# RWKV mixer: whole-bank transposes of k, b and the output rows, and a reordered tail

## What is computed

```
def step(state, inp):                     # one token t of each of 16 heads of width 64
    r_t, w_t, k_t, v_t, a_t, b_t = inp
    sa = einsum('bhvk,bhk->bhv', state, a_t)
    state = state * w_t + sa[..., None] * b_t + v_t[..., None] * k_t
    y_t = einsum('bhvk,bhk->bhv', state, r_t)
...
y = group_norm(y) * ln_w + ln_b + bonus   # per head
return (y * g) @ w_o                      # g = sigmoid(xg @ g1) @ g2
```

## Time and profile before

| | us |
|---|---|
| runs of the kernel before | 1758.68, 1757.01, 1758.20 |
| their median | 1758.20 |
| the profiled execution | 1757.71 |
| its span in the trace | 1755.1 |
| the RWKV stage from x to the last group of w_o in that span | 1437.7 to 1561.7 |

### The profile page before, as it was taken

The page is one execution under the profiler, slowest core; times in us unless marked ns, Lnnn a source line. Parts: engine busy times, 40 slices in busy tenths (PEclk is TensorE's granted clock), DMA queues, the critical chain, the costliest instruction groups (busy, mean ns, idle before and its releaser), DMA issues.

```text
span 1755.1 us, 33424 instructions
## 1 busy us (share of the span) xinstructions
PE 1728.4 (98%) x12454; PEld 1523.5 (87%) x12454; DVE 1003.2 (57%) x1927; ACT 945.6 (54%) x1414; POOL 1133.0 (65%) x506
## 2 busy tenths in 40 slices
PE   8999999999999999999999999999999999999998
PEld 6888899999999999888888887988888989978887
DVE  5224333992478888544444446465555985665555
ACT  5468454446544444455444456666657762346565
POOL 6966776887888888655555556755566463555553
PEclk9999999999999999999999999999999999999999
DMA  8543443665544444566667763455544521245552
GB/s 303 195 157 130 159 173 141 184 184 181 175 148 141 140 143 143 168 192 192 192 207 253 242 191 108 169 216 192 191 150 138 178 63 52 66 156 194 190 190 83
DMA packets 68094, 292.57 MB, mean 167 GB/s; under 512 B 13184, under 2 KB 13712, under 8 KB 50464
## 3 DMA queue, kind: packets, MB, share of 16 engines
q1 hardware_dynamic: 67808, 291.12, 50.8%
q0 software_dynamic: 48, 0.08, 0.0%
q10 hardware_dynamic: 144, 0.07, 0.0%
HBM read 289.14 MB, written 1.05 MB: 165 GB/s over the span
## 4 chain that ended last, share of the span: by engine, by line
PE 80%; POOL 9%; issue 5%; ACT 2%; DVE 2%; DMA 1%; POOLq 0%; DVEq 0%; SPq 0%; ACTq 0%
PE bank L1060 8%; POOL rows_lo L2983 7%; PE bank L876 7%; PE bank L1081 6%; PE bank L938 6%; PE bank L941 6%; PE bank L935 6%; PE bank L1196 4%; PE bank L1064 4%; PE bank L882 4%; PE bank L618 4%; PE bank L624 4%; PE bank L619 4%; PE bank L908 3%; PE bank L647 1%
## 5 line engine op out<-in xcount | busy, mean ns | idle before, releaser
L2968 POOL TENSOR_TENSOR unit_lo<-unit_raw,unit_hi 128x2048 fp32r<-128x2048 f32 (+1 forms) x86 | 332.9, 3886 | 132.4 <-ACT unit_hi L1649 119.6
L2983 POOL TENSOR_TENSOR rows_lo<-rows_raw,rows_hi 128x1024 fp32r<-128x1024 f32 x128 | 309.6, 2420 | 84.8 <-ACT rows_hi L1769 46.0
L3010 POOL TENSOR_TENSOR a_lo<-table,a_hi 128x256 fp32r<-128x256 f32 x128 | 178.7, 1396 | 159.7 <-ACT a_hi L1848 159.6
L2567 DVE TENSOR_TENSOR rows_lo<-rows_raw,rows_hi 128x1024 fp32r<-128x1024 f32 x128 | 161.8, 1264 | 185.5 <-ACT rows_hi L1844 185.5
L1844 ACT ACTIVATE rows_hi<-rows_raw 128x1024 fp32r<-128x1024 f32 x128 | 135.6, 1060 | 168.4 <-PE bank L941 168.4
L3040 POOL TENSOR_TENSOR up_lo<-up_raw,up_hi 128x2048 fp32r<-128x2048 f32 x22 | 111.2, 5054 | 156.5 <-ACT up_hi L1920 126.9
L1649 ACT ACTIVATE unit_hi<-unit_raw 128x2048 fp32r<-128x2048 f32 x70 | 134.0, 1918 | 65.4 <-PE bank L624 36.9
L1060 PE MATMUL bank<-x_lo_hi,up_hi 128*128 128x512 f32 x640 | 159.8, 392 | 0.4 <-DVE acc L2660 0.4
L882 PE MATMUL bank<-x_lo_hi,rows_lo 128*128 128x256 f32 x1024 | 143.2, 282 | 0.5 <-POOL rows_lo L2983 0.5
L882 PEld LDWEIGHTS bank<-x_lo_hi,rows_lo 128*128 128x128 f32 x1024 | 135.7, 190 | 6.6 <-POOL rows_lo L2983 0.9
L938 PE MATMUL bank<-rows_hi,a_lo 128*128 128x512 f32 x512 | 138.5, 391 | 0.8 <-POOL a_lo L3010 0.8
(11 more groups left out here) (491 smaller groups left out, 3929.2 us busy)
## 6 DMA issues: line engine op xcount, KB each, us to landing
unit_raw<-in_ring SPq DMA_DIRECT2D x70, 1024.0 KB, 5.0
rows_raw<-in_u SPq DMA_DIRECT2D x128, 512.0 KB, 3.6
rows_raw<-in_v SPq DMA_DIRECT2D x128, 512.0 KB, 3.6
up_raw<-in_up SPq DMA_DIRECT2D x44, 1024.0 KB, 5.2
down_raw<-in_down SPq DMA_DIRECT2D x22, 1024.0 KB, 4.9
unit_raw<-in_ring SPq DMA_DIRECT2D x20, 256.0 KB, 3.6
const<-in_const SPq DMA_DIRECT2D x1, 1792.0 KB, 15.0
X<-in_x SPq DMA_DIRECT2D x2, 512.0 KB, 5.7
```

Source lines behind the costliest of these rows:

```text
L2567: V.tensor_tensor(rows_lo[q][:, :], rows_raw[q][:, :], rows_hi_f[q % 2], ALU.subtract).then_inc(S("v_lo_ready"), 1)
L2968: return nc.gpsimd.tensor_tensor(unit_lo[SLOT_OF[n]][:, w], unit_raw[SLOT_OF[n]][:, w], hi, ALU.subtract)
L2983: nc.gpsimd.tensor_tensor(rows_lo[q][:, :], rows_raw[q][:, :], rows_hi_f[q % 2], ALU.subtract).then_inc(S("u_lo_ready"), 1)
L3010: nc.gpsimd.tensor_tensor(a_lo[q % 2][:, :], table[:, i * ROWS_RING + q, :], a_hi_f[q % 2], ALU.subtract).then_inc(S("a_lo_ready"), 1)
```

## The change

- `by_token` no longer makes two groups of 16 products per chunk. It turns 128x128 blocks, which hold two chunks at once, by transposes: four per bank, two banks for b of chunks 0 and 1 (`bt0`), two for k of them (`kt0`), and the same for chunks 2 and 3 (`bt1`, `kt1`). The eight groups become four calls of eight transposes.
- ScalarE copies such a bank in four pieces of 64 partitions x 256 elements, since one bank now holds two chunks and both heads. Of each call there are 8 pieces. They stand behind x2 (`bt0`), behind y8 (`kt0`), behind y8 of chunk 3 (`bt1`) and behind y_ of chunk 1 (`kt1`).
- `turned` is eight 128x128 transposes per half of the tokens. They put features on other partitions than before, so the rows of w_o are loaded in that order (each of 16 loads now 64 partitions x 2 runs) and the columns of g2 too (four loads in runs of 64 elements, 256 bytes, for one load of whole rows).
- `turned(0)` moves ahead of the last two groups of y_ of chunk 3. `turned(1)` moves into the first half of the tokens, ahead of the last group of `out_rows(1, 0)`.
- On VectorE `yg_of(0)` moves ahead of the sum over y_ of chunk 3. On GpSimd the lo part of WO+2 moves ahead of `rows_centred(2)`.

```diff
-            def by_token(c):
-                products(("bt", c), b_of(c), ident_of)
-                products(("kt", c), k_of(c), ident_of)
+            def by_token(n, t):
+
+                for i in range(2):
+                    o = fill((n, i))
+                    for j in range(4):
+                        at_ = slice(j * P, (j + 1) * P)
+                        last = nc.tensor.transpose(o[:, at_], t[:, 4 * i + j, P * int(n[2]):P * int(n[2]) + P], ident)
+                    full((n, i), last)
 
             def bonus_sums(c):
...
             def step_add(c):
-                made(c, "kt", "bt")
+                for n in ("kt", "bt"):
+                    for i in range(2):
+                        wait_drained(pe, (n + str(c // 2), i))
                 o = fill(("ds", c), 2)
                 add_products(o, kt_of(c), v_of(c), closed=False, last=False)
                 made(c, "u")
...
             first = range(3)
             for c in first:
                 x_of_chunk(c)
-            by_token(0)
+            by_token("bt0", aaT)
             for c in first:
                 squares(c, c)
-            by_token(1)
             for c in first:
                 fourths(c, c)
+            by_token("kt0", kfT)
             for c in first:
                 eighths(c, c)
...
             step_rhs(0)
-            by_token(2)
+            by_token("bt1", aaT)
             squares(c, 0)
             step_u(0)
...
             inverse(c, 0)
-            by_token(c)
+            by_token("kt1", kfT)
             step_u(2)
             bonus_sums(c)
...
-            step_out(3, state=False)
-
-
             def turned(th):
 
                 pe.wait_ge(S("ys_ready"), 2 + th)
                 if th:
                     wait_drained(pe, ("y_", NRC - 1))
                 for b in range(2):
-                    o = fill(("yt", th, b), 2)
-                    ends = [None, None]
-                    for j in range(4):
+                    o = fill(("yt", th, b))
+                    by_tile = o[:, :].rearrange("p (i q h t) -> p i h q t", i=2, q=2, h=2)
+                    for i in range(2):
                         for half in range(2):
-                            for par in range(2):
-                                r = head(par)
-                                at_ = j * P + half * RCH
-                                ends[par] = mm(o[r, at_:at_ + RCH], ys[r, 2 * th + half, 4 * b + j, :], ident[r, r], start=True, stop=True)
-                    full_by_heads(("yt", th, b), ends)
-
-            def out_rows(j, c):
+                            t = nc.tensor.transpose(by_tile[:, i, half, :, :], ys[:, 2 * th + half, 4 * b + 2 * i:4 * b + 2 * i + 2, :], ident)
+                    full(("yt", th, b), t)
+
+            def out_rows(j, c, before_last=None):
 
                 o = fill(("wo2", j, c))
...
                         mm(o[:, :], tokens(yg_lo, k), hi[:, k, :], start=False, stop=False)
+                    if half and before_last:
+                        before_last()
                     wait_lo()
                     for k in range(4):
                         t = mm(o[:, :], tokens(yg_hi, k), lo[:, k, :], start=False, stop=half == 1 and k == 3)
...
-            for th in range(2):
-                turned(th)
-                plan.next = 2 * th
-                for j in range(2):
-                    out_rows(j, th)
+            step_out_state(3)
+            step_u(3)
+            turned(0)
+            step_out(3, state=False)
+            plan.next = 0
+            out_rows(0, 0)
+
+            def turn_the_others():
                 plan.next = 5
+                turned(1)
+
+            out_rows(1, 0, turn_the_others)
+            plan.next = 2
+            for j in range(2):
+                out_rows(j, 1)
+            plan.next = 5
             if upto < 8:
                 return
...
                         sp.dma_start(raw[DK * i:DK * i + DK, 0:D], src[0:DK, D * i:D * i + D]).then_inc(raw_loaded[SLOT_OF[n]], 16)
+                elif n == UNIT_AT["GATE2"]:
+                    for h in range(2):
+                        for par in range(2):
+                            dst = raw[:, :].rearrange("p (i q h v) -> p i q h v", i=8, q=2, h=2)[:, :, par, h, :]
+                            sp.dma_start(dst, src.rearrange("p (i h q v) -> p i h q v", i=8, h=2, q=2)[:, :, h, par, :]).then_inc(raw_loaded[SLOT_OF[n]], 16)
                 elif n >= UNIT_AT["WO"]:
                     for i in range(4):
                         if after:
                             wait_filled(sp, after[i])
-                        w = slice(512 * i, 512 * i + 512)
-                        sp.dma_start(raw[:, w], src[:, w]).then_inc(raw_loaded[SLOT_OF[n]], 16)
+                        h, par = i // 2, i % 2
+                        by_heads = lambda t: t.rearrange("p (i q n) -> p i q n", i=2, q=2)
+                        sp.dma_start(by_heads(raw[:, :])[head(h), :, par, :], by_heads(src)[head(par), :, h, :]).then_inc(raw_loaded[SLOT_OF[n]], 16)
                 else:
                     sp.dma_start(raw[:, :], src).then_inc(raw_loaded[SLOT_OF[n]], 16)
...
 
-            def by_token(c):
-                copies([c], "bt", kept(btok))
-                copies([c], "kt", kept(ktok))
+            def by_token(n, dst):
+
+                for i in range(2):
+                    o = wait_filled(act, (n, i))[:, :].rearrange("p (m q v) -> p m q v", m=4, q=2)
+                    for half in range(2):
+                        for par in range(2):
+                            t = A(dst[2 * int(n[2]) + half][head(par), 4 * i:4 * i + 4, :], o[head(half), :, par, :], ACT.Copy)
+                    drain((n, i), t)
 
             def bonus_sums(c):
                 o = wait_filled(act, ("bo", c))
                 drain(("bo", c), A(bonus[:, c, :], o[:, 0:PAIRS], ACT.Copy))
 
-            by_token(0)
             copies(first, "x2", of(m_x2))
-            by_token(1)
+            by_token("bt0", btok)
             copies(first, "x4", of(m_x4))
             eighths(first)
+            by_token("kt0", ktok)
             copies(first, "mT", of(m_y2))
             copies(first, "nT", of(m_x4))
             for c in first:
                 bonus_sums(c)
             last = range(NRC - 1, NRC)
-            by_token(2)
             copies(last, "x2", of(m_x2))
             copies(last, "x4", of(m_x4))
             eighths(last)
+            by_token("bt1", btok)
             out_rows(0)
             units_ahead(UNIT_AT["WO"])
             copies(last, "mT", of(m_y2))
...
             out_rows(1)
-            by_token(NRC - 1)
+            by_token("kt1", ktok)
             bonus_sums(NRC - 1)
             out_rows(2)
...
                 wait_drained(ve, ("g2", b))
+            yg_of(0)
             o = eight(wait_filled(ve, ("y_", c)))
             V.tensor_reduce(each(64, c), o, AX, ALU.add).then_inc(S("rows_mean_ready"), 1)
-            yg_of(0)
             ve.wait_ge(S("rows_mean_ready"), c + 1)
             V.scalar_tensor_tensor(o, bc(each(64, c).unsqueeze(2), [PAIRS, DK]), -1.0 / DK, o, ALU.mult, ALU.add).then_inc(S("rows_mean_ready"), 1)
             yg_lo_of(0)
...
                     rows_shift((0, NRC - 1)[c])
-                if c != 1:
-                    units_lo(UNIT_AT["WO"] + (2, 0, 3, 4)[c])
+                if c != 2:
+                    units_lo(UNIT_AT["WO"] + (2, 3, 0, 4)[c])
             if upto >= 8:
```

More of the change, by code:

```diff
@@ L408, in wait_loaded @@
         same = [m for m in range(n + 1) if SLOT_OF[m] == SLOT_OF[n]]
-        eng.wait_ge(raw_loaded[SLOT_OF[n]], 16 * sum(2 if m in (UNIT_AT["LORA1"], UNIT_AT["LORA2"]) else 4 if m >= UNIT_AT["WO"] else 1 for m in same))
+        eng.wait_ge(raw_loaded[SLOT_OF[n]], 16 * sum(2 if m in (UNIT_AT["LORA1"], UNIT_AT["LORA2"]) else 4 if m >= UNIT_AT["GATE2"] else 1 for m in same))
     def wait_released(eng, n):
@@ L1369, in _ @@
             plan.next = plan.at[("y_", 2)][0]
-            step_out_state(3)
-            step_u(3)
-            step_out(3, state=False)
             def turned(th):
@@ L1566, in _ @@
                 wait_filled(sp, ("tt", NRC - 2))
-                after = [("bo", 0), ("bo", 1), ("bo", 2), ("x", 3, 0), ("x", 3, 1), ("rhs", 0), ("bt", 2), ("kt", 2), ("x2", 3), ("u", 0), ("x4", 3), ("r2", 3)]
+                after = [("bo", 0), ("bo", 1), ("bo", 2), ("x", 3, 0), ("x", 3, 1), ("rhs", 0), ("bt1", 0), ("bt1", 1), ("x2", 3), ("u", 0), ("x4", 3), ("r2", 3)]
                 for n in range(3):
@@ L2067, in _ @@
             of = lambda t: lambda c: t[lane(c)][:, :, :]
-            kept = lambda t: lambda c: t[c][:, :, :]
             def out_rows(c):
```

## The result

| | us |
|---|---|
| runs of the changed kernel | 1763.87, 1762.60, 1764.13, 1766.70, 1766.01 |
| their median | 1764.13 |
| runs of the kernel before beside them | 1758.68, 1757.01, 1758.20, 1758.27, 1757.77; median 1758.20 |
| ratio, 95% interval | 1.0042 [1.0031, 1.0053] |
| span of the profiled execution | 1762.1, before 1755.1 |

The change makes the kernel slower: by 0.42% in the ratio, by 5.9 us (0.34%) in the two medians. I had forecast no change, 1756.9, and at most 1759.8.

The account below looks back on a forecast made before the run. The stage was taken as bound by PE's own list. +1.5 for `by_token` and -2.8 for the tail made -1.3: 1757.71 to 1756.4, plus 0.5 for the median, 1756.9 us; range 1754.5 to 1759.8.

Parts of the forecast that it names:

- The third squares: Head of the stage: they start at 1447.29 as before, set by VectorE, so 0.95 us saved on chunk 0 is lost.
- The waits for ktok and btok: PE idles 1.1 to 1.3 us before r4 of chunks 0 and 1, about 2 before r3 and y_.
- GATE2 is not late: GATE2 load lands near 1417, 13 us before g2 needs it; the rival that it is late had 0.02.
- The unit_lo wait: Tail, `out_rows(1, 0)`: PE's 0.90 us wait for GpSimd's unit_lo of WO+3 goes, as that ends at 1543.7.
- +1.5 for `by_token`: Chunk 3: waits for late bt1 pieces put y_ of chunk 0 1.5 us behind, kept to the stage's end.
- -2.8 for the tail: Tail: the second half of the tokens starts at 1547.7 instead of 1550.49, 2.8 us ahead.
- Price of a piece on ScalarE: ScalarE's 64x256 copies: pitch 0.27 us, bounds 0.27 and 0.40; eight pieces last 2.27 us.
- Loads: Turned loads: GATE2 lands 13 us early and w_o is read long after, so costed at nothing.
- end within the time of that wait: Before ds of chunk 2: kt1's eight pieces finish while ds waits for u from VectorE anyway.
- the slowing of VectorE by GpSimd: Tail rival: both working on SBUF slow each other; half the gain, 1.4, gives 1758.3; chance 0.11.
- dear pieces: Rival: ScalarE pieces cost more; 1759.8 at 0.40 us each (chance 0.13), 1761.7 at 0.48 (past 0.40, chance 0.10).

Follow-up runs that it names:

- token_only: The kernel before with the new `by_token` and its ScalarE pieces, old loads and old tail: 1764.10 us, ratio 1.0046.
- tail_only: The changed kernel with the old `by_token`, keeping the turned rows, their loads and the reordered tail: 1756.68 us, ratio 1.0001.
- tail_plain_pool: The changed kernel with old `by_token`, both loads in whole rows and GpSimd's old order (lo part of WO+2 behind the rows of chunk 2): 1754.05 us, ratio 0.9984.
- tail_plain_loads: The changed kernel with the old `by_token` and the loads of w_o and GATE2 in whole rows: 1756.73 us, ratio 1.0002.
- tail_wo_turned: The changed kernel with the old `by_token` and GATE2 in whole rows, only w_o loaded in the turned form: 1756.62 us, ratio 0.9997.
- tail_g2_turned: The changed kernel with the old `by_token` and w_o in whole rows, only GATE2 loaded in the turned form: 1755.99 us, ratio 0.9995.
- act_early: The changed kernel with ScalarE's pieces of kt0 ahead of y8 and of bt1 ahead of x4 of chunk 3: 1758.92 us, ratio 1.0012.
- one late call at a time: Two kernels, each token_only with one call's pieces moved earlier on ScalarE: only kt0's late 1759.49 us, only bt1's late 1760.62 us.
- old_pieces_late: The kernel before, bt and kt of chunk 2 copied in eight 64x256 pieces within a half, behind y8 of chunk 3: 1760.91 us, ratio 1.0019.
- loads_plain: The changed kernel with the loads of w_o and g2 in whole rows, the host laying the weights out in the new order: 1763.65 us, ratio 1.0040.

## Why the prediction was wrong

**Right.** The third squares stay bound by VectorE and the first transposes gain nothing (1.08 instead of 0.38 of idle). The waits for ktok and btok stand at r4 of chunks 0 and 1 and at r3 of chunk 3. `by_token` of eight transposes has a pitch of 1.02 (0.92 taken). GATE2 is not late: its loads land 4.6 us after their issue, and g2 starts at 1428.90, 1.82 earlier like the rest. The unit_lo wait is gone, and `turned(1)` waits for nobody.

**Which terms failed.** The sum was +1.5 for `by_token` and -2.8 for the tail. token_only measures the first term as +7.3, tail_only the second as -0.1. Both were wrong: the first in the price of a piece (0.27 for 0.39), in kt1's wait (none for 1.5) and in a clock that I took to be constant, the second in the 0.69 that I left to VectorE beside GpSimd (1.63 to 1.75 measured).

**Where the time is.** Against my own times (shifted by the 1.82 of the start), 10.2 us are missing at the end of the stage, 1568.62 for 1558.41:

- *The step "Price of a piece on ScalarE".* I gave a 64x256 the overlap of 0.11 that copies of 128x512 have, and so 0.27, with 379 ns in the earlier trace rows and 0.40 in the earlier trace rows before me. It is 0.39, crossing or not. r4 of chunk 1 starts at 1462.14 for 1460.68, 1.5 late: 0.84 by this price and the rest by the transposes (0.1 more than I took), an idle 0.25 where bt0's bank is asked for, and smaller pauses. The estimate of 0.306 that I drew from the Trainium skill (ScalarE: Activation LUTs, "What ACT_TABLE_LOAD costs") is low as well; the measurement decides.
- *What a wait does to the clock* was in no step. The profile of before holds such a spell, behind 1.70 us of idle time at 1336.91, and I didn't look for it because the stage itself had 1.00 throughout. y_ of chunk 0 is another 4.8 late: the gap of 3.17, the piece price 0.84, and 0.8 for one group at half clock.
- *The step "Loads".* "Costed at nothing": in the profile with both loads turned PE is idle for 3.17. The medians put it between 0 and 2.1.
- *kt1 "end within the time of that wait".* They don't. ds of chunk 2 is idle 1.48 before, and falls another 1.2 back.
- *The tail* is 2.8 later than the forecast: one more spell (1529 to 1532, 1.6 us) and the wait of 2.26, less some waits that the forecast already had there (0.35 for u in ds of chunk 2, some 0.5 before `turned(0)`). My own working put unit_lo of WO+2 on GpSimd from 1529.27 on and rows_scaled of chunk 1 on VectorE from 1529.30 to 1530.71, side by side, and left that at 0.69. I had named the slowing of VectorE by GpSimd as a rival, but at unit_lo of WO+3; the rows of before at 1541.48 and 1542.55 have its price. The 2.8 that I forecast for the tail is there with GpSimd's old order (tail_plain_pool, 3.0 below before). That the sizes agree is luck, since the forecast had the new order in it. The order of the diff leaves 0.1 to 1.1 of it (tail_only, tail_plain_loads, tail_wo_turned, tail_g2_turned).

The rival "dear pieces" held the right mechanism and was not enough alone. By its own slopes it is worth 2.8 us at 0.39 (the prediction dropped the first 0.16 in its sums: 2.9 should be 3.0, 4.8 should be 5.0, and the 0.6 for a pitch of 0.306 should be 0.8); the late pieces make 3.8 (act_early) to 5.5 us (one late call at a time), a good part of it by the clock.

## What to carry to other kernels

Read the price of a small ScalarE instruction as its full length unless a run of the same shape shows an overlap. When an edit makes PE wait in a stretch where it was always busy, add to the wait the chance of a spell at half clock behind it: in old_pieces_late waits of 2.5 us cost 3.3 to 3.9. Before moving GpSimd work, look what VectorE does at that time, and above all whether it reads both inputs from SBUF; and a move on one engine's list helps only if the engine that ends last is moved too (kt1).

## What the runs showed of the hardware

- Every spell within the stage, in every profile that has one, lasted 3.4 us, but for the first one of the change with 6.8. One spell costs 1.6 to 1.7 us of progress where PE is busy (3.62 for 2.03 in token_only, 8.83 for 7.14 at 1338 us of before). It also comes where PE has no wait: in 9 of the 18 profiles it begins in or up to 1.2 us behind the bonus sums, a run of products of one column each. PE's windows there in tail_plain_loads:

```profile
1480.00:1481.00 1.00, 1.00 (x40) 1.00 0.36 94
1481.00:1482.00 1.00, 1.00 (x21) 0.80 0.51 166
1482.00:1483.00 1.00, 1.00 (x14) 0.50 0.69 207
...
1484.00:1485.00 1.00, 1.00 (x23) 0.50 0.77 262
1485.00:1486.00 1.00, 1.00 (x40) 0.99 0.66 217
```

- Whether it comes varies from run to run of one kernel: the runs of the kernel before have mean clocks from 0.996 on and times from 1754.2 to 1759.8. One profile can therefore show a difference that the medians do not bear out (loads_plain: span 3.4 shorter than that of the change, medians 0.5 apart).
- The two operations of rows_scaled that take both inputs from SBUF, on 128x512, took 0.69 alone and 1.03 to 1.75 beside GpSimd's unit_lo, in every profile; those that read a PSUM bank beside it kept 0.70 (1544.36 in the kernel before). GpSimd's four pieces of unit_lo took 5.8 to 5.9 where both operations ran beside them and 5.0 to 5.1 elsewhere.
